# The first panel of the second output projection is accumulated inside the attention mixer's last turns, and the mixer's follow-up products come one turn later

## The chip, the cores and the metric

One of the cores of a Trainium2 chip runs the whole program. The metric is the device time of one execution in microseconds (us). TensorE (PE) does the matrix products and transposes, ScalarE (ACT), VectorE (DVE) and GpSimd (POOL) the rest, and SyncE (SP) issues most transfers. Each engine takes its instructions in the written order and waits on semaphores.

## The reference

One inference step of a decoder with two layers, for a prompt of 1024 tokens and a group of 8 sequences with 4 new tokens each (1056 tokens in all, 1024 features).

```
layer 0: h += mlstm(rmsnorm(h)) @ w_out_a        ; h += relu(rmsnorm(h) @ w_up)^2 @ w_down
k, v = rmsnorm(h) @ w_kv                         (16 heads of 64, shared)
layer 1: q = rmsnorm(h) @ w_q_b
         z = q k^T / 8 + bias, causal, strictly  (prompt: 1024 new keys;
                                                  sample: 1024 paged keys and 4 new ones)
         a[t,s] = sigmoid(z[t,s]) * prod over s<j<t of (1 - sigmoid(z[t,j]))
         y = a v ; h += y @ w_out_b              ; h += relu(rmsnorm(h) @ w_up)^2 @ w_down
y = rmsnorm(h)
```

The change touches the attention of layer 1 (the second mixer) and `y @ w_out_b`.

## The kernel before, in words

Every activation is kept with a feature to a partition, [128, 8, 1056] in float32: `m.h` is the residual, later the mixer's output y. A dense product is made from three float32r matmuls: operand and weight are each split into a high part (a cast, `w_hi`, `x_hi`) and a low part (the difference, `w_lo`, `x_lo`), and hi*hi, hi*lo and lo*hi are added up in PSUM. A weight panel has 128 output features and 1024 inputs: `load_panel` brings it into one of two buffers `w_raw`, `split_panel` (POOL, L162 and L164) splits it. A panel is worked on in three tiles of 352 tokens, each of 8 x 3 = 24 matmuls.

**`mixer_b`** (L1348) goes over 8 pairs of heads. A pair has 8 slots (`SLOTS`), one for each tile of 128 query rows, the largest first; slot number 8p+n is slot n of pair p, pairs and slots being counted from 0. In each slot PE runs `turns`: first `z(p, n, 0)` (scores of both heads, L1592 and the mask L1596), then the turns that `turns_of` lists. A turn is a set of transposes into bank 5 or 6 in alternation (`turn`), which ACT then copies out (`read_turn`); with it goes a product that uses the copy (`follow`). The kinds are "page" (cached keys, transposes L1623; after the fourth page the sample group's scores, L1673), "pack" (weights a, transposes L1642; then the product with the values, L1688), "sat" (the sample group's weights, L1649), "new", "values", "keys" and "ys" (the sample group's y, L1655). `turn` waits until the turn two before it was read. After a turn comes a part of the next pair's projections (`third`, L1576 to L1578: 6 or 9 matmuls of 352 columns), as many per slot as `THIRDS_AT` says and none in the last pair, after the second turn `z(p, n, 1)` where the tile has a second chunk, and then `follow` of the turn before. In slots 1 and 5 the product of cached values with the sample weights comes in four quarters (`values`, L1702; the last also L1707): after the turns 0, 1 and 3 and at the end of the slot. SP loads the pages into a ring of 8 buffers, in the order of their use, and each load waits until PE has used the page 8 loads ago.

ACT makes the gates of each chunk and head, two sigmoids (`gates`, L1774 and L1775), between the copies of the turns in a written order: one `gates` after each turn. It may start a slot's gates when DVE has done the last slot's. DVE (`chain_of`) does for each chunk two running products (scan, L1915) and two products of SBUF with SBUF (L1921); the sample group has its own (`chain_sample`, L1930 and L1934, in slots 3, 4, 7 and 0). PE's packs of slot n are in slot n+1 and wait for these (`a_ready`). `run_out` (L1939) copies the finished y tile from PSUM into `m.h`.

After its last slot the mixer has on SP `head_loads` (the first two panels of w_out_b) and on POOL `head_splits`.

**`out_and_mlp`** (L1978) follows behind a barrier of all engines. It splits y: for each of its 8 feature blocks k a cast on ACT (L2088) and a difference on DVE (L2142). PE waits for block k and does panel 0 (`out_matmuls`, 72 matmuls, L2032 to L2034), then the panels 1 to 7 tile by tile. ACT, after the casts, brings back the residual that had been spilled, block by block (L2092, `h_back`), and DVE adds each tile to it (L2148). Between two panels' sums DVE also adds up squares (`norm_add`) and makes the low part of the next operand (`x_low`), each after a step of ACT. A tile of panel n starts when the sum of the same tile of panel n-1 has been read (`tile_free`).

## Time and profile before

| | us |
|---|---|
| median of 3 runs | 2983.94 |
| lowest and highest | 2976.22, 2984.82 |
| the profiled execution, its own time | 2977.9 |
| its span | 2976.1 |
| PE busy | 2847.8 (96%) |
| DVE busy | 1303.7 (44%) |
| ACT busy | 819.4 (28%) |
| POOL busy | 731.6 (25%) |

All instants below are us from the start of the span of this one execution. The second mixer's pairs start at 1363.8 and the last of them at 2034.1; PE ends the mixer at 2111.1. A group of instructions is shown with its count, its busy time, the mean of one in ns, and the idle time of its engine just before it with what ended that. Matmuls overlap, so that one of 352 columns lasts some 323 ns but the next starts about 160 ns later.

### The profile page before, as it was taken

Reading aid. Unit: us, or ns where it says so; the run is one execution under the profiler, and the core shown is the slowest. Engines: PE = TensorE matmul, PEld = TensorE weight load, DVE = VectorE, ACT = ScalarE, POOL = GpSimd, SP = SyncE. Lnnn points to the kernel's source line nnn. Section 1 sums busy time; section 2 is a strip of 40 time slices with the busy share of each in tenths; the row PEclk is TensorE's granted clock in tenths of the full one; section 3 lists DMA queues with packets and bytes.
Section 4 is the critical chain, followed back from the end, with each engine's and each line's share of the span. In section 5 each row is a group of like instructions: output and inputs, shape, how many; then the busy total and the mean of one; then the engine's idle time right before and its main releaser. Section 6 shows DMA issues by size and latency. Waiting matters only on the chain. (4 is left out here: it accounts for less than half of the span.)

```text
span 2976.1 us, 49009 instructions
## 1 busy us (share of the span) xinstructions
PE 2847.8 (96%) x19713; PEld 2609.5 (88%) x19713; DVE 1303.7 (44%) x1851; ACT 819.4 (28%) x1675; POOL 731.6 (25%) x449
## 2 busy tenths in 40 slices
PE   7999998999999999999999999998899999999998
PEld 6988887999999999986777677665799999999997
DVE  6323345433333333355556655565543333333334
ACT  5221123201110011125555655556320111001112
POOL 3222102223232232322112111210222323223231
PEclk9999998999999999999999999999899999999999
DMA  5575524222323223234343443434311111111112
GB/s 164 187 148 187 100 30 102 92 86 86 98 85 99 85 89 94 86 103 120 113 121 107 115 128 108 121 101 114 123 50 43 44 49 42 49 42 47 45 43 79
DMA packets 361448, 277.23 MB, mean 93 GB/s; under 512 B 31379, under 2 KB 352915, under 8 KB 359251
## 3 DMA queue, kind: packets, MB, share of 16 engines
q1 hardware_dynamic: 340074, 261.97, 30.3%
q10 hardware_dynamic: 21224, 13.15, 2.3%
q8 instruction: 108, 1.77, 0.3%
q14 instruction: 42, 0.34, 0.0%
HBM read 251.06 MB, written 91.11 MB: 115 GB/s over the span
## 5 line engine op out<-in xcount | busy, mean ns | idle before, releaser
L162 POOL CAST w_hi<-w_raw 128x1024 fp32r<-128x1024 f32 x193 | 206.2, 1068 | 1606.8 <-PE bank L214 904.6
L212 PE MATMUL bank<-p_u_hi,w_hi 128*128 128x352 f32 x1536 | 496.6, 323 | 7.2 <-DVE p_u_lo L2166 5.8
L212 PE MATMUL bank<-x_hi,w_hi 128*128 128x352 f32 x1536 | 496.0, 323 | 1.7 <-PEq L2256 1.7
L213 PE MATMUL bank<-p_u_lo,w_hi 128*128 128x352 f32 x1536 | 495.7, 323 | 0.0
L214 PE MATMUL bank<-p_u_hi,w_lo 128*128 128x352 f32 x1536 | 495.5, 323 | 0.0
L214 PE MATMUL bank<-x_hi,w_lo 128*128 128x352 f32 x1536 | 493.8, 321 | 0.0
L213 PE MATMUL bank<-x_lo,w_hi 128*128 128x352 f32 x1536 | 493.2, 321 | 0.0
L164 POOL TENSOR_TENSOR w_lo<-w_raw,w_hi 128x1024 fp32r<-128x1024 f32 x193 | 468.2, 2426 | 15.5
L2116 ACT ACTIVATE p_u_hi<-p_relu 128x352 fp32r<-128x352 f32 x192 | 95.7, 499 | 1207.0 <-DVE p_relu L2163 1207.0
L2172 DVE TENSOR_TENSOR h<-bank,h 128x352 f32<-128x352 f32 x384 | 198.6, 522 | 467.1 <-PE bank L214 467.1
L2166 DVE TENSOR_TENSOR p_u_lo<-p_relu_sq,p_u_hi 128x352 fp32r<-128x352 f32 x192 | 229.1, 1193 | 182.7 <-ACT p_relu_sq L2117 182.7
L212 PEld LDWEIGHTS bank<-p_u_hi,w_hi 128*128 128x128 f32 x1536 | 288.4, 188 | 12.2 <-issue 10.0
L212 PEld LDWEIGHTS bank<-x_hi,w_hi 128*128 128x128 f32 x1536 | 288.5, 188 | 3.6 <-issue 3.6
L213 PEld LDWEIGHTS bank<-x_lo,w_hi 128*128 128x128 f32 x1536 | 289.3, 188 | 0.0
L214 PEld LDWEIGHTS bank<-x_hi,w_lo 128*128 128x128 f32 x1536 | 288.6, 188 | 0.0
L213 PEld LDWEIGHTS bank<-p_u_lo,w_hi 128*128 128x128 f32 x1536 | 288.5, 188 | 0.0
L214 PEld LDWEIGHTS bank<-p_u_hi,w_lo 128*128 128x128 f32 x1536 | 288.5, 188 | 0.0
L1915 DVE TENSOR_TENSOR_SCAN square<-square,zero 128x512 f32<-128x512 f32 (+5 forms) x192 | 217.9, 1149 | 150.5 <-ACT square L1775 149.1
L2163 DVE SCALAR_TENSOR_TENSOR p_relu<-bank,rms_inverse 128x352 f32<-128x352 f32 x192 | 100.0, 521 | 270.9 <-PE bank L214 263.5
L812 PE MATMUL bank<-x_hi,w_hi 128*128 128x352 f32 x576 | 200.7, 348 | 5.3 <-DVE p_v_next L1155 2.5
L814 PE MATMUL bank<-x_hi,w_lo 128*128 128x352 f32 x576 | 186.3, 323 | 0.0
L813 PE MATMUL bank<-x_lo,w_hi 128*128 128x352 f32 x576 | 186.1, 323 | 0.0
(271 smaller groups left out, 4426.6 us busy)
## 6 DMA issues: line engine op xcount, KB each, us to landing
k_pages<-in_cache_k SPq DMA_DIRECT2D x64, 512.0 KB, 5.9
w_raw<-in_w_up SPq DMA_DIRECT2D x64, 512.0 KB, 4.0
v_pages<-in_cache_v SPq DMA_DIRECT2D x64, 512.0 KB, 4.7
w_raw<-in_w_down SPq DMA_DIRECT2D x64, 512.0 KB, 3.4
p_pages<-k_pages SPq DMA_DIRECT2D x256, 128.0 KB, 2.4
p_pages<-v_pages SPq DMA_DIRECT2D x256, 128.0 KB, 2.4
w_raw<-in_w_in_a SPq DMA_DIRECT2D x25, 512.0 KB, 4.1
h_spill<-h SPq DMA_DIRECT2D x16, 528.0 KB, 5.2
```

Source lines behind the costliest of these rows:

```text
L162: pool.tensor_copy(m.whi[slot][:, :], m.wraw[slot][:, :]).then_inc(w.hi, 1)
L164: pool.tensor_tensor(m.wlo[slot][:, :], m.wraw[slot][:, :], f32(m.whi[slot][:, :]), ALU.subtract)\
L212: pe.matmul(bank[:, 0:TW], wh, xh, start=(k == 0), stop=False)
L213: pe.matmul(bank[:, 0:TW], wh, xl, start=False, stop=False)
L214: last = pe.matmul(bank[:, 0:TW], wl, xh, start=False, stop=(k == nk - 1))
L812: pe.matmul(bank[:, 0:TW], wh, xh, start=(kk == 0), stop=False)
L813: pe.matmul(bank[:, 0:TW], wh, xl, start=False, stop=False)
L814: last = pe.matmul(bank[:, 0:TW], wl, xh, start=False, stop=(kk == KT - 1))
L1915: dve.tensor_tensor_scan(stick, stick, m.zero[:, 0:1].broadcast_to([P, hi - lo]), sticks[h2][:, hi:hi + 1] if x else 1.0, ALU.mult, ALU.ad ...
L2163: dve.scalar_tensor_tensor(out=relu[t][:, :], in0=m.bank[t][:, 0:TW], scalar=0.0, in1=m.rs[:, toks], op0=ALU.max, op1=ALU.mult).then_inc(w ...
L2166: dve.tensor_tensor(ulo[:, u, toks], sqr[t][:, :], f32(uhi[:, u, toks]), ALU.subtract)\
L2172: dve.tensor_tensor(ht, m.bank[t][:, 0:TW], ht, ALU.add).then_inc(w.tile_free[t], 1)
```

## The change

In the mixer:
- `follow` of a turn comes one turn later (a list `pending`, emptied by `settle`): after the transposes of the turn two behind it. One is carried over into the next slot, behind its `z`.
- The quarters 0 and 1 of `values` both come after turn 0 of slots 1 and 5; quarter 3 goes into the next slot, after turn 1. ACT's `gates_sample` and `rows_sample` move with this.
- `head_loads` on SP moves from the end to slot 3 of the last pair (slot number 59), ahead of that slot's page loads.
- POOL, once DVE has done slot 2 of the last pair, splits w_out_b's panel 0, then the y blocks of pairs 0 to 6 (`split_y`: a cast and a difference of 128 x 1056 each, put into halves of `x_hi` and `x_lo`), then panel 1.
- PE does, for k = 0 to 6, panel 0's 9 matmuls each (`out_first`): the tiles 0 and 1 behind the last 7 turns (from turn 3 of slot 61 on), the tile 2 at the ends of the last two slots, after bank 2 is free.

In `out_and_mlp`, for the second layer alone (`begun`): PE starts with panel 1, blocks 0 to 3, in banks 3 to 5; then block 7 of panel 0; then blocks 4 to 7 of panel 1. ACT and DVE split y only for the blocks 7, 4, 5 and 6.

```
+def early_place(k):
+    return (k + KT // 2) % KT
...
-    VALUES_AFTER = {0: [0], 1: [1], 3: [2]}
+    VALUES_AFTER = {0: [0, 1], 3: [2]}
+    LAST_VALUES_AT, LAST_AFTER = {2: 0, 6: 1}, 1
...
+    OUT_FROM, OUT_K = SLOTS * (PAIRS - 1) + 5, PAIRS - 1
+    OUT_LAST_TILE = {SLOTS * PAIRS - 1: range(0, 3), SLOTS * PAIRS: range(3, OUT_K)}
...
+    OUT_SKIP = sum(len(turns_of(s)) for s in range(OUT_FROM, LAST)) - OUT_K
...
+        after = m.heads[3]
+        y_hi, y_x = own.sem("y_hi_ready"), own.sem("y_split")
...
+                if slot == OUT_FROM - 2:
+                    head_loads(eng, m, after, w, 3 * PAIRS)
                 used = len(at(KEYS_AT, slot)) * 2 * SG + len(at(VALUES_AT, slot)) * SG * QUARTERS
...
-            head_loads(eng, m, m.heads[3], w, 3 * PAIRS)
...
-            head_splits(pool, m, m.heads[3], w, (TILES * PAIRS - NT, TILES * PAIRS))
+            def split_out(slot):
+                pool.wait_ge(after.w.loaded[slot], 16)
+                split_panel(pool, m, after.w, slot, slot, None)
+            def split_y(k):
+                hi, lo = m.xhi[:, early_place(k), :], m.xlo[:, early_place(k), :]
+                pool.wait_ge(y_ok, (k + 1) * SLOTS)
+                pool.wait_ge(turn_read, TURN_NO["ys", k, 1] + 1)
+                pool.tensor_copy(hi, m.h[:, k, :]).then_inc(y_hi, 1)
+                pool.wait_ge(y_hi, k + 1)
+                pool.tensor_tensor(lo, m.h[:, k, :], f32(hi), ALU.subtract).then_inc(y_x, 1)
+            pool.wait_ge(w.tile_ready, TILES * PAIRS)
+            pool.wait_ge(a_ready, unit_no(PAIRS - 1, 3, 0, 0))
+            split_out(0)
+            for k in range(OUT_K):
+                split_y(k)
+            split_out(1)
...
+            pending = []
+            def settle(left):
+                while len(pending) > left:
+                    follow(pending.pop(0))
+            def out_first(k, tiles):
+                pe.wait_ge(y_x, k + 1)
+                if k == 0:
+                    pe.wait_ge(after.w.split, 1)
+                    pe.wait_ge(w.tile_free[0], TILES * PAIRS)
+                wh, wl = m.whi[0][:, k * P:(k + 1) * P], m.wlo[0][:, k * P:(k + 1) * P]
+                for t in tiles:
+                    bank, ts = m.bank[t][:, 0:TW], slice(t * TW, (t + 1) * TW)
+                    xh, xl = m.xhi[:, early_place(k), ts], m.xlo[:, early_place(k), ts]
+                    pe.matmul(bank, wh, xh, start=(k == 0), stop=False, skip_group_check=True)
+                    pe.matmul(bank, wh, xl, start=False, stop=False, skip_group_check=True)
+                    pe.matmul(bank, wl, xh, start=False, stop=False, skip_group_check=True)
...
-                quarters = [(q, g, x) for q, g in at(VALUES_AT, slot) for x in range(QUARTERS)]
+                outs = sum(len(turns_of(x)) for x in range(OUT_FROM, slot)) - OUT_SKIP
+                quarters = [(q, g, x) for q, g in at(VALUES_AT, slot) for x in range(QUARTERS - 1)]
                 tiles = 0 <= p < PAIRS
                 lower = tiles and len(CHUNKS[n]) > 1
                 if tiles:
                     z(p, n, 0)
-                before = None
+                settle(0)
                 for i, y in enumerate(turns_of(slot)):
                     turn(y)
+                    settle(1)
+                    pending.append(y)
                     if fill:
                         third(p, d)
                         d, fill = d + 1, fill - 1
+                    if slot >= OUT_FROM and outs + i >= 0:
+                        out_first(outs + i, (0, 1))
                     if i == 1 and lower:
                         z(p, n, 1)
-                    if before is not None:
-                        follow(before)
-                    before = y
                     for x in VALUES_AFTER.get(i, ()):
                         if x < len(quarters):
                             values(*quarters[x])
+                    if i == LAST_AFTER:
+                        for q, g in at(LAST_VALUES_AT, slot):
+                            values(q, g, QUARTERS - 1)
                 while fill:
                     third(p, d)
                     d, fill = d + 1, fill - 1
-                if before is not None:
-                    follow(before)
+                for k in OUT_LAST_TILE.get(slot, ()):
+                    if k == 0:
+                        pe.wait_ge(ys_read, PAIRS * 2)
+                    out_first(k, (2,))
+                settle(1 if 0 <= slot < SLOTS * PAIRS - 1 else 0)
                 if len(turns_of(slot)) < 2 and lower:
                     z(p, n, 1)
...
-                    if i and turns[i - 1][0] == "page" and turns[i - 1][2][2] == SG - 1:
-                        gates_sample(turns[i - 1][1], *turns[i - 1][2][:2])
+                    if i == LAST_AFTER + 1 - (turns[LAST_AFTER + 1:][:1] in [[("ys", q, g)] for q, g in at(LAST_VALUES_AT, slot)]):
+                        for q, g in at(LAST_VALUES_AT, slot):
+                            rows_sample(q, g)
+                    if i >= 2 and turns[i - 2][0] == "page" and turns[i - 2][2][2] == SG - 1:
+                        gates_sample(turns[i - 2][1], *turns[i - 2][2][:2])
                 if slot == EARLY:
...
-                if turns and turns[-1][0] == "page" and turns[-1][2][2] == SG - 1:
-                    gates_sample(turns[-1][1], *turns[-1][2][:2])
+                for y in turns[-2:]:
+                    if y[0] == "page" and y[2][2] == SG - 1:
+                        gates_sample(y[1], *y[2][:2])
                 for x, h2 in due:
                     gates(p, n, x, h2)
-                for q, g in at(VALUES_AT, slot):
-                    rows_sample(q, g)
...
-def out_and_mlp(nc, m, own, w_out, w_up, w_down, gain, gather, head, after, norm_after):
...
+        if begun:
+            yhi = [m.xhi[:, early_place(k), :] for k in range(HALF)] + [uhi[:, k - HALF, :] for k in range(HALF, KT)]
+            ylo = [m.xlo[:, early_place(k), :] for k in range(HALF)] + [ulo[:, k - HALF, :] for k in range(HALF, KT)]
+            y_order = [KT - 1] + list(range(HALF, KT - 1))
+        else:
+            yhi = [uhi[:, k, :] for k in range(HALF)] + [m.xhi[:, k, :] for k in range(HALF, KT)]
+            ylo = [ulo[:, k, :] for k in range(HALF)] + [m.xlo[:, k, :] for k in range(HALF, KT)]
+            y_order = list(range(KT))
+        def out_bank(n, t):
+            return m.bank[3 + t if begun and n == 1 else t][:, 0:TW]
...
-            pe.wait_ge(w.split, 1)
-            for k in range(KT):
-                pe.wait_ge(y_x, k + 1)
+                check = dict(skip_group_check=True) if begun and n == 0 else {}
+                pe.matmul(out_bank(n, t), wh, yhi[k][:, ts], start=(k == 0), stop=False, **check)
+                pe.matmul(out_bank(n, t), wh, ylo[k][:, ts], start=False, stop=False, **check)
+                return pe.matmul(out_bank(n, t), wl, yhi[k][:, ts], start=False, stop=(k == KT - 1), **check)
+            if begun:
+                pe.wait_ge(w.split, 2)
+                for k in range(HALF):
+                    for t in range(NT):
+                        out_matmuls(1, k, t)
+                pe.wait_ge(y_x, 1)
                 for t in range(NT):
-                    last = out_matmuls(0, k, t)
-                    if k == KT - 1:
-                        last.then_inc(w.tile_ready, 1)
-            for n in range(1, KT):
+                    out_matmuls(0, KT - 1, t).then_inc(w.tile_ready, 1)
+                pe.wait_ge(y_x, KT - HALF)
+                for t in range(NT):
+                    for k in range(HALF, KT):
+                        last = out_matmuls(1, k, t)
+                    last.then_inc(w.tile_ready, 1)
+            else:
+                pe.wait_ge(w.split, 1)
+                for k in range(KT):
+                    pe.wait_ge(y_x, k + 1)
+                    for t in range(NT):
+                        last = out_matmuls(0, k, t)
+                        if k == KT - 1:
+                            last.then_inc(w.tile_ready, 1)
+            for n in range(2 if begun else 1, KT):
                 pe.wait_ge(w.split, n + 1)
                 for t in range(NT):
...
-            for k in range(KT):
+            for k in y_order:
                 act.activation(yhi[k], m.h[:, k, :], ACT.Copy).then_inc(y_hi, 1)
             for k in range(KT):
-                act.wait_ge(y_x, k + 1)
+                if k in y_order:
+                    act.wait_ge(y_x, max(y_order.index(x) for x in y_order if x <= k) + 1 if begun else k + 1)
                 act.dma_start(m.h[:, k, :], m.spill[k]).then_inc(h_back[k], 16)
...
-            for k in range(KT):
-                dve.wait_ge(y_hi, k + 1)
+            for i, k in enumerate(y_order):
+                dve.wait_ge(y_hi, i + 1)
                 dve.tensor_tensor(ylo[k], m.h[:, k, :], f32(yhi[k]), ALU.subtract).then_inc(y_x, 1)
...
-                    dve.tensor_tensor(ht, m.bank[t][:, 0:TW], ht, ALU.add).then_inc(w.tile_free[t], 1)
+                    dve.tensor_tensor(ht, out_bank(k, t), ht, ALU.add).then_inc(w.tile_free[t], 1)
...
         phase(mixer_b)
-        phase(out_and_mlp, d["w_out_b"][0], d["w_up"][1], d["w_down"][1], m.g_mlp[1], False, m.heads[3], None, 0)
+        phase(out_and_mlp, d["w_out_b"][0], d["w_up"][1], d["w_down"][1], m.g_mlp[1], False, m.heads[3], None, 0, True)
```

## Rows read from the trace of the kernel before

**Rows 1.** The page's part 1: TensorE, its busy time, share of the span, instructions

```profile
PE 2847.8 (96%) x19713; PEld 2609.5 (88%) x19713; DVE 1303.7 (44%) x1851; ACT 819.4 (28%) x1675; POOL 731.6 (25%) x449
```

**Rows 2.** Busy time by stretch: length, then each engine's busy us (instructions); clock, DMA share, GB/s

```profile
1363.80:2034.10 670.30, 637.08 (x5542) 478.13 (x5538) 388.15 (x522) 378.86 (x797) 109.83 (x60) 1.00 0.41 117
...
2069.80:2111.20 41.40, 28.35 (x277) 17.07 (x275) 25.22 (x35) 23.15 (x54) 7.12 (x4) 0.91 0.34 95
...
2115.50:2141.20 25.70, 25.68 (x146) 25.62 (x147) 14.13 (x15) 7.56 (x8) 3.45 (x2) 0.90 0.58 210
...
2109.20:2120.40 11.20, 6.23 (x23) 5.49 (x24) 6.69 (x8) 9.05 (x10) 0.00 (x0) 0.50 0.64 202
```

**Rows 3.** TensorE's waits, pairs 0 to 6 (1363.8 to 2034.1): us, times, longest

```profile
PE bank L1688 <- ACT p_weights_t L1827: 17.6, 35, 1.0
PE bank L1702 <- DMA p_pages<-v_pages: 6.1, 7, 1.4
PE bank L1623 <- ACT p_page_keys_t L1811: 4.3, 7, 0.6
PE bank L1673 <- ACT p_page_keys_t L1811: 4.0, 7, 0.6
```

**Rows 4.** TensorE's waits in slot 2 of pair 6 (1961.7 to 1976.2)

```profile
PE bank L1688 <- ACT p_weights_t L1827: 1.1, 2, 0.8
```

**Rows 5.** ScalarE in slot 2 of pair 6, in order of time: start, duration, instruction

```profile
1968.83 0.71 ACT L1774 ACTIVATE p_weights<-bank,p_bias 128x512 f32<-128x512 f32 x1
...
1969.98 0.61 ACT L1811 COPY p_page_keys_t<-bank 128x512 f32<-128x512 f32 x1
```

**Rows 6.** GpSimd in order of time where both engines had work queued (1298 to 1305)

```profile
1298.97 1.84 POOL L162 CAST w_hi<-w_raw 128x1024 fp32r<-128x1024 f32 x1 [0.17 <-POOL w_raw L158]
1300.90 3.29 POOL L164 TENSOR_TENSOR w_lo<-w_raw,w_hi 128x1024 fp32r<-128x1024 f32 x1
```

**Rows 7.** VectorE in the same stretch

```profile
1299.84 2.08 DVE L295 TENSOR_TENSOR squares<-squares,square 128x1056 f32<-128x1056 f32 x1
```

**Rows 8.** VectorE in slot 63 (2103.3 to 2109.1), under GpSimd's two panel splits

```profile
2103.35 2.17 DVE L1915 TENSOR_TENSOR_SCAN square<-square,zero 128x127 f32<-128x127 f32 x1
...
2106.55 2.37 DVE L1921 TENSOR_TENSOR p_weights<-p_weights,square 128x127 f32<-128x127 f32 x1
```

**Rows 9.** VectorE by shape, 2066.3 to 2100.8, no GpSimd work: count, busy, mean ns

```profile
L1915 DVE TENSOR_TENSOR_SCAN square<-square,zero 128x511 f32<-128x511 f32 x4 | 4.9, 1243 | 2.0 <-ACT square L1775 2.0
L1915 DVE TENSOR_TENSOR_SCAN square<-square,zero 128x383 f32<-128x383 f32 x2 | 1.9, 956 | 2.7 <-ACT square L1775 2.7
L1930 DVE TENSOR_TENSOR_SCAN squares<-squares,zero 128x544 f32<-128x544 f32 x1 | 1.3, 1284 | 0.0
...
L1921 DVE TENSOR_TENSOR p_weights<-p_weights,square 128x511 f32<-128x511 f32 x2 | 1.3, 676 | 0.0
...
L1921 DVE TENSOR_TENSOR p_weights<-p_weights,square 128x127 f32<-128x127 f32 x2 | 0.5, 275 | 0.0
```

**Rows 10.** GpSimd's panel splits by line, 2120 to 2600

```profile
L164 POOL TENSOR_TENSOR w_lo<-w_raw,w_hi 128x1024 fp32r<-128x1024 f32 x41 | 98.6, 2404 | 3.3
L162 POOL CAST w_hi<-w_raw 128x1024 fp32r<-128x1024 f32 x41 | 42.6, 1039 | 346.0 <-PE bank L214 217.7 <-issue 83.2 <-PE bank L2034 45.1
```

**Rows 11.** SyncE's issues around slots 58 and 63, and a panel's time to landing

```profile
2068.01 0.58 SPq L1542 DMA_DIRECT2D out_v_sample<-p_v_rows  x1
...
2095.69 1.87 SPq L130 DMA_DIRECT2D w_raw<-in_w_out_b  x2
...
w_raw<-in_w_out_b SPq DMA_DIRECT2D x2, 512.0 KB, 5.8
```

**Rows 12.** The start of the output projection: PE's first matmul, panel 1's last sum, reload

```profile
2115.52 0.63 PE L2032 MATMUL bank<-p_u_hi,w_hi 128*128 128x352 f32 x1 [4.44 <-DVE p_u_lo L2142]
...
2141.19 0.52 DVE L2148 TENSOR_TENSOR h<-bank,h 128x352 f32<-128x352 f32 x1 [3.33 <-PE bank L2034]
...
h<-h_spill ACTq DMA_DIRECT2D x8, 528.0 KB, 5.5
```

9 lines of the change are left out of this document (3 added, 6 removed).

## The prediction

> **What bounds the kernel now.** I read the busy times first. TensorE is busy for 96% of the span [rows 1], so a gain must come from its idle time, from its clock, or from fewer matmuls, and none are removed here: they move. So I read by stretch [rows 2]. In the mixer's pairs 0 to 6 PE is busy 637.1 of 670.3 us: 33 us idle, nearly all of it the 32.0 us of waits listed in [rows 3], 4.6 a pair. From slot 3 of the last pair to the mixer's end it is busy only 28.4 of 41.4 us. Behind that end it stands 4.44 us until the first y block is split [rows 12], and up to 2120.4 its granted clock is 0.50, the 1.2 GHz level [rows 2]. These are the two places that the change aims at. The third view is of DVE and POOL, which make what PE would wait for next.
>
> **Part 1, the order in pairs 0 to 6.** Each group of waits asks: what is late when the waiting product is moved back?
> The DMA wait (6.1 us in 7 pairs, 0.9 each [rows 3]) is the last quarter of the cached values in slot 1. It moves behind two turns of slot 2, some 3 us later, and its pages are asked for at the same time as before or earlier. It goes: -0.9. The next key pages are released later for it, but come in 2.5 us and are due about 3 us after. I cost that at nothing; if that cover is short, up to 1 us a pair returns.
> The waits on ACT (17.6 + 4.3 + 4.0 [rows 3], 3.7 a pair) go only in part. The transposes two turns on need the same copy read as `follow` does, so the wait moves to them unless PE has more work in between or ACT is faster. In slot 2, with 1.1 us of these [rows 4] and 0.6 of L1623, ACT goes through copy, gates, copy in the written order: the gates of 1968.83 stand ahead of the copy of 1969.98 that PE waits for [rows 5]. This order stays. What PE gains is the 0.6 us of a `follow` and 1 us of the moved quarter as filling, less a `rows_sample` of 0.3 us now in ACT's queue there: I take -0.7 of 1.7. Slot 3 has most of the rest of the L1688 waits, 1.2 us, behind the same kind of gates: -0.1. In slot 6 turns with only copies on ACT lie between; its 0.8 us (0.6 of L1673, 0.2 of L1688) nearly goes: -0.7. Against it, the sample scores of pages now come after the next slot's `z`, so their gates delay the slot's own on ACT by 1 us, and `z(p, 0, 1)` waits for these: +0.3.
> Sum: -0.9 - 0.7 - 0.1 - 0.7 + 0.3 = -2.1 a pair, seven times **-15 us**. The bounds: the DMA wait alone, -6, and all waits, -32. I stay near the lower, since ACT's order decides and is not changed where most of the wait is.
>
> **Part 2, POOL's work in the last pair.** This costs more than it seems. Where DVE and POOL both have work, they take turns: POOL's cast from 1298.97 lasts 1.84 us instead of 1.04 [rows 6, 10], DVE's sum from 1299.84 lasts 2.08 and ends at 1301.92 [rows 7], 1.1 us after that cast, and POOL's difference from 1300.90 lasts 3.29 instead of 2.40: it began in earnest when DVE's sum ended. It holds for the scans too: in slot 63 a scan of 127 columns takes 2.17 us and a product 2.37 where products of this width take 0.28 [rows 8, 9], each ending as POOL's instruction ends. Copies out of PSUM aren't held.
> The Trainium skill, SBUF — State Buffer, section "Who interferes with whom", states the same as a lock held for the whole instruction, by any VectorE operation with two SBUF inputs against a GpSimd one that reads SBUF. By that rule the new work could not hide beside DVE's, only in its gaps; the rows agree.
> POOL starts when w_out_b's panel 0 has landed. SP comes to it after the store of 2068.01, so at 2068.6, and a panel takes 5.8 us [rows 11]: 2074.4. Its two issues, 1.9 us, stand ahead of slot 3's page loads, which have to wait for PE's page turns about as long anyway: nothing, or 1 us if not. From there POOL has 2 panels at 1.04 + 2.40 us and 7 y blocks, 1056 columns wide instead of 1024, at 1.07 + 2.48 [rows 10]: 6.9 + 24.9 = 31.7 us. DVE has, from the second chunk of slot 3 to the end of slot 62's chain, 10 scans and 10 products: 4 scans of 511 columns at 1.24, 2 of the sample group at 1.28, 2 of 383 at 0.96 and 2 of 255 at about 0.7, 10.8 us; the products lie between 0.68 and 0.28, some 5.9 in all [rows 9]. Of these 16.7 us neighbouring records overlap by about 0.1 each, so 14.7 us of holding. Both in turn: 2074.4 + 31.7 + 14.7 = 2120.8. Slot 62's chain ended just before 2103.35 [rows 8]: 17 us later. DVE's gaps don't save this: POOL always has the next instruction ready, and 31.7 + 14.7 us exceed the 29 us there were.
> What follows on the end of that chain: before 7.8 us (2103.3 to 2111.1), of which POOL's panels cost 4 [rows 8] that is now gone. New on this path are matmuls. Of the 63 moved, at 0.16 us, 10.1 us in all, most stand where PE waits anyway; but the 6 and 12 of slot 64 (2.9 us) and a few in slot 62, with the moved quarter and the copy that the "ys" turn then waits for, come after the last chains: +4.5. PE's new waits on y blocks (`y_x`) cost nothing, since POOL is through with a block before DVE has the chain that the same turn needs. The two pieces cancel nearly; the earlier slots of the pair gain 0.8 by part 1's order. Last pair: **+17 us**, with bounds of +3 (all of POOL's work in gaps: only the tail's matmuls) and +22 (every POOL instruction on the path).
> The clock: it fell to 0.50 around waits of 3.4 and 4.4 us at the end [rows 2, 12]. Now PE waits about 4 us twice in slots 60 to 62, and works 20 us in between; I take 5 to 6 us of that work at the half clock with half of it on the path: **+3** (0 to +10).
>
> **Part 3, the projection's start.** Before: from PE's last mixer matmul at 2111.1 (2115.52 less 4.44) to the end of panel 1 at 2141.1 [rows 12] 30.0 us: the wait, 144 matmuls at 0.16, and 2.4 for the slow clock. After: the barrier, 0.6, then 36 + 9 + 36 = 81 matmuls, 13.0: the needed y block 7 is split after 3 us, beside these. The four casts and four differences of y that ACT and DVE no longer make lay beside PE's work: nothing. That alone gives 13.6. But next is late the residual. Its reload is issued only behind four casts, about 5.9 us after the mixer, and takes 5.5 [rows 12]: 11.4. Then DVE has 3 sums of 0.52, ACT a square, DVE an addition and a low part, some 5 us, before panel 1's first sum frees the tile that panel 2 waits for: 17.1. Part 3: 17.1 - 30.0 = **-13 us**; bounds -16.4 (nothing late) and -11.
>
> **Sum.** -15 + 17 + 3 - 13 = -8 us. Against the profiled execution, 2977.9 us, that is 2970; against the median of the runs, 6 us higher, 2976.
>
> **The rivals.**
> A, POOL's work hides. If DVE regains its delays in the 16 us for which it is idle in the last 41 [rows 2], the pair grows by some 5 instead of 20: -15 + 5 - 13 = -23, 2961. For it: DVE does wait for ACT and PE there. Against it: the sum above leaves no gap unused. 0.18.
> B, the order pays more. If two further copies' waits go in slots 2 and 3, part 1 is -25: 2966. For it: PE gets one more turn's work before each wait. Against it: ACT's gates stand between. 0.12.
> C, slower. The last pair starves PE so long that its clock stays at the half level from slot 60 into the projection. Then the 25 us of PE work there take up to twice as long and cover DVE no more: +10 on top of +3, and if the order gives just the DMA waits, -6: -6 + 17 + 13 - 13 = +11, 2995. It decides from about 10 us of half clock on the path. For it: the clock fell after waits of this size. 0.15.
> D, part 1 does not do what it says: the waits move to the transposes entire, and the key pages' wait replaces the values'. Then 0 + 17 + 3 - 13 = +7, 2991. 0.10.
> The forecast has 0.45, over some 2969 to 2984.
>
> **How the numbers follow.** A measurement of this kernel tells 0.3%, 9 us, from no change: faster is below 2975, slower above 2993. Of the forecast's 0.45 I count 0.15 as faster and 0.30 as same; A and B are faster (0.30); C is slower (0.15); D lies by the edge, 0.07 same and 0.03 slower. Faster 0.45, same 0.37, slower 0.18. The range, 2957 to 2996, takes in A, B, D and most of C.
>
> **What would show it.** Right: PE's waits in pairs 0 to 6 near 17 us, no L1702 wait on DMA, L1642 or L1623 in its place; POOL busy without a break from about 2060 on for 45 us; scans and products of slots 59 to 62 at 2 to 3 us; the last pair 90 us and more long; panel 2 of the projection waiting for `tile_free`. Wrong: the last pair under 82 us, or scans that keep their 1.2 us beside POOL; waits of pairs 0 to 6 below 8 us or above 26.

## The result and the profile after

| | before | after |
|---|---|---|
| median of 4 runs, us | 2981.93 | 2949.96 |
| lowest and highest, us | 2976.22, 2984.82 | 2949.24, 2953.85 |
| the profiled execution, its own time, us | 2977.9 | 2949.79 |
| its span, us | 2976.1 | 2948.0 |

The ratio is 0.9898, with a 95% interval of 0.988 to 0.9916. The kernel is faster by 1%, some 30 us. The prediction gave "faster" a chance of 0.45; its 2976 us and its range from 2957 us on both miss: every term of the sum came out lower, none above what was forecast.

In the stretches of the prediction, each cut at the same instruction in both traces (the first `z` of pair 0, that of pair 7, PE's last product of the mixer, the first matmul of the projection's panel 2), in us:

| stretch | before | after | difference | predicted |
|---|---|---|---|---|
| ahead of the second mixer's pairs | 1363.8 | 1361.6 | -2.2 | 0 |
| pairs 0 to 6 | 670.3 | 647.3 | -23.0 | -15 |
| last pair | 77.0 | 89.6 | +12.6 | +17 and +3 |
| mixer's end to panel 2 | 29.9 | 14.1 | -15.8 | -13 |
| the rest | 827.0 | 827.3 | +0.3 | 0 |

The stretches sum to the difference of the spans, 28.1 us. The first one is no effect: over the traces of all kernels of this case it lies between 1361.0 and 1366.2 with nothing in it changed.

One of these boundaries does not part the same work in both kernels. The `follow` that is now carried over a slot's end takes 8 matmuls (sample scores, 1.0 us) from pair 6 into pair 7. Before, they start ahead of the boundary (2034.1), and after, behind it (2008.9):

```profile
2033.12 1.06 PE L1673 MATMUL bank<-p_page_keys_t,p_q_sample 128*32 128x512 f32 x8
```

```profile
2010.16 1.07 PE L1704 MATMUL bank<-p_page_keys_t,p_q_sample 128*32 128x512 f32 x8
```

So 1.0 us of the -23.0 is not saved but stands in the last pair, and the same work changed by -22.0 and +11.6.

Part 1 of the page of after:

```profile
PE 2839.9 (96%) x19713; PEld 2610.2 (89%) x19713; DVE 1343.1 (46%) x1847; ACT 815.7 (28%) x1671; POOL 766.3 (26%) x463
```

Its busy time by stretch, with the columns of [rows 2]:

```profile
1361.60:2008.90 647.30, 631.38 (x5536) 480.76 (x5532) 411.09 (x520) 378.50 (x797) 110.11 (x60) 1.00 0.42 120
2008.90:2098.50 89.60, 68.58 (x597) 43.77 (x596) 69.47 (x66) 48.04 (x103) 40.62 (x18) 0.90 0.31 86
2098.50:2112.60 14.10, 13.24 (x82) 12.92 (x82) 10.16 (x12) 7.45 (x7) 3.45 (x2) 1.00 0.85 306
```

The matmuls are the same 19713 as in [rows 1]. PE's idle time of pairs 0 to 6 halved, from 33.2 us [rows 2] to 15.9. In the last pair POOL is busy for 40.6 us, and VectorE's busy time is 69.5 us. The same 66 instructions take 48.9 us in a kernel without the y splits on POOL (order alone, below). The projection's start has hardly any idle time left and the full clock, where [rows 2] had 0.50.

PE's waits in pairs 0 to 6 after, with the columns of [rows 3]:

```profile
PE bank L1654 <- ACT p_page_keys_t L1872: 7.1, 14, 0.8
PE bank L1673 <- ACT p_weights_t L1888: 6.9, 7, 1.0
PE bank L1623 <- ACT square L1836: 1.6, 6, 0.3
PE bank L1733 <- DMA p_pages<-v_pages: 0.2, 1, 0.2
```

L1654 are the transposes of pages (L1623 before), L1673 those of the weights (L1642 before), L1623 the scores (L1592 before), L1733 the cached values (L1702 before). The 17.6 us of `follow` (L1688 [rows 3]) and the DMA wait are gone; what remains stands on transposes and scores. It is 15.8 us in all.

### The profile page after: what moved, and what is told of

It reads as the page before. It is cut to its first block and busy times, and to the rows that moved or that the text cites. A ratio compares the mean times of both kernels' runs of the same rounds, so it can differ in the third digit from the quotient of the medians.

```text
span 2948.0 us, 49024 instructions
## 1 busy us (share of the span) xinstructions
PE 2839.9 (96%) x19713; PEld 2610.2 (89%) x19713; DVE 1343.1 (46%) x1847; ACT 815.7 (28%) x1671; POOL 766.3 (26%) x463
## 5 line engine op out<-in xcount | busy, mean ns | idle before, releaser
L212 PEld LDWEIGHTS bank<-p_u_hi,w_hi 128*128 128x128 f32 x1536 | 288.7, 188 | 12.2 <-issue 10.0
L1978 DVE TENSOR_TENSOR_SCAN square<-square,zero 128x512 f32<-128x512 f32 (+5 forms) x192 | 240.9, 1277 | 92.3 <-ACT square L1836 92.0
```

The source lines that it names most:

```text
L212: pe.matmul(bank[:, 0:TW], wh, xh, start=(k == 0), stop=False)
L1978: dve.tensor_tensor_scan(stick, stick, m.zero[:, 0:1].broadcast_to([P, hi - lo]), sticks[h2][:, hi:hi + 1] if x else 1.0, ALU.mult, ALU.ad ...
```

## The experiments

The edits are against the changed kernel, but for loads early, which is against the kernel before. A comparison with the kernel before is with runs on the same chip. The stretches were cut as above, in one trace for each kernel. "Lower clock" is the time in the last pair for which PE was granted the lower level (1.2 GHz, 0.50 in the rows); what PE does in it would take half as long at the full one, so that a difference in this column is a rival for a part of a difference in the column before it.

| kernel | median | ratio to before, 95% | pairs 0 to 6 | last pair | lower clock | to panel 2 |
|---|---|---|---|---|---|---|
| before | 2981.9 to 2983.9 | | 670.3 | 77.0 | 17.9 | 29.9 |
| after | 2949.96 | 0.988 to 0.9916 | 647.3 | 89.6 | 17.1 | 14.1 |
| order alone | 2955.73 | 0.9892 to 0.9925 | 647.8 | 78.0 | 15.6 | 29.4 |
| panel alone | 2979.76 | 0.9981 to 1.0 | 673.7 | 90.9 | 23.9 | 14.1 |
| part ahead of `follow` | 2951.01 | 0.9877 to 0.991 | 646.1 | 89.5 | 17.1 | 14.2 |
| quarters back | 2969.21 | 0.9938 to 0.9973 | 661.8 | 92.1 | 23.9 | 14.1 |
| last quarter back | 2961.82 | 0.9896 to 0.9939 | 655.0 | 92.6 | 23.9 | 14.2 |
| y splits of 8 columns | 2942.56 | 0.9847 to 0.9887 | 647.3 | 78.5 | 6.8 | 14.1 |
| loads early | 2981.22 | 0.9981 to 1.0 | 671.3 | 75.6 | 17.1 | 29.2 |
| y splits sooner | 2962.86 | 0.991 to 0.9946 | 647.3 | 101.9 | 37.5 | 14.1 |
| y splits in halves | 2948.94 | 0.9867 to 0.9904 | 647.3 | 85.6 | 17.1 | 14.2 |
| cast by ACT | 2951.53 | 0.9863 to 0.9914 | 647.3 | 91.6 | 23.9 | 14.2 |
| y splits by ACT and DVE | 2948.16 | 0.9847 to 0.9892 | 647.4 | 85.6 | 17.1 | 14.2 |
| and panels later | 2946.47 | 0.9863 to 0.9896 | 647.7 | 83.3 | 17.1 | 14.2 |
| and one y moved | 2946.64 | 0.9862 to 0.9895 | 647.3 | 82.2 | 13.7 | 14.1 |

**One part each.** The order alone leaves out the panel's part:

```
-                if slot == OUT_FROM - 2:
-                    head_loads(eng, m, after, w, 3 * PAIRS)
...
+            head_loads(eng, m, m.heads[3], w, 3 * PAIRS)
...
-            split_out(0)
-            for k in range(OUT_K):
-                split_y(k)
-            split_out(1)
+            head_splits(pool, m, m.heads[3], w, (TILES * PAIRS - NT, TILES * PAIRS))
...
-                    if slot >= OUT_FROM and outs + i >= 0:
-                        out_first(outs + i, (0, 1))
...
-        phase(out_and_mlp, d["w_out_b"][0], d["w_up"][1], d["w_down"][1], m.g_mlp[1], False, m.heads[3], None, 0, True)
+        phase(out_and_mlp, d["w_out_b"][0], d["w_up"][1], d["w_down"][1], m.g_mlp[1], False, m.heads[3], None, 0, False)
```

> Part 1 alone: the turn order, the quarters and ScalarE's order as in the changed kernel; w_out_b's first panels, the y splits and panel 0 as in the kernel before. Theory 1 (the gain is the order's; the early panel gives back in the last pair what it takes from the projection): 25 to 30 us below the kernel before, so about 2953, pairs 0 to 6 in 647 us as in the changed kernel, the last pair 72 to 75. Theory 2 (each part pays about half, as the change is laid out): 12 to 18 us below, about 2966, since without the early panel the gain of 16 us at the projection's start is missing.

Measured: 2955.73 us, and 647.8 us for pairs 0 to 6. The order gives all of that stretch's gain, as the first theory has it. The last pair is 1.0 us longer, neither 72 to 75 us nor 0.8 shorter as forecast; the 8 matmuls that now lie behind the boundary are that 1.0 us.

The panel alone has the old order of `follow`, `values` and the gates:

```
-    VALUES_AFTER = {0: [0, 1], 3: [2]}
+    VALUES_AFTER = {0: [0], 1: [1], 3: [2]}
...
-                    settle(1)
-                    pending.append(y)
                     if fill:
                         third(p, d)
...
                     if i == 1 and lower:
                         z(p, n, 1)
+                    settle(0)
+                    pending.append(y)
...
-                settle(1 if 0 <= slot < SLOTS * PAIRS - 1 else 0)
+                settle(0)
```

> Part 2 alone: the order of turns, follow-ups and quarters as in the kernel before; the head loads in slot 59, the y splits on GpSimd, panel 0 in the last turns and the new start of the projection as in the changed kernel. Theory 1: within 5 us of the kernel before: pairs 0 to 6 at 670 us, the last pair 13 to 17 us longer (90 to 94), the projection's start 16 shorter. Theory 2: 10 to 16 us below it.

Measured: 2979.76 us, within 5 us of the kernel before, as in the first theory. The projection's start pays 15.8 us, the last pair takes 13.9 of it back, and what is left is not told from nothing (0.9981 to 1.0). Pairs 0 to 6 are 3.4 us longer here. PE was at the lower level for 10.2 us of them, where before was for 3.4, which makes 3.4 us if PE was busy throughout, as it was:

```profile
1363.10:2036.90 673.80, 640.19 (x5544) 480.95 (x5540) 387.69 (x522) 379.51 (x797) 109.79 (x60) 0.99 0.41 116
```

**What in the order pays.** Three edits. First, the `third` ahead of the `follow` again, everything else as in after:

```
-                    settle(1)
-                    pending.append(y)
                     if fill:
                         third(p, d)
...
                     if slot >= OUT_FROM and outs + i >= 0:
                         out_first(outs + i, (0, 1))
+                    settle(1)
+                    pending.append(y)
```

> The changed kernel, but the follow-up product (still two turns late) stands behind the part of the projections instead of ahead of it. In pairs 0 to 6 TensorE's waits fell by 16 us and the time by 23. Theory 1 (the other 7 us are the order of matmul shapes: a follow-up behind a part starts 0.25 us after its predecessor, one behind a transpose 0.20, and a part behind a transpose has a slow second matmul): pairs 0 to 6 take 5 to 7 us more, 652 to 654, with waits unchanged near 16 us. Theory 2 (the 7 us are waits that the profile doesn't list): no change, 645 to 649.

Measured: 646.1 us against 647.3, with the waits on ACT the same to a tenth. Which of the two comes first is not the reason.

Second, all quarters of `values` and the copy of the sampled rows go back to their old places:

```
-    VALUES_AFTER = {0: [0, 1], 3: [2]}
+    VALUES_AFTER = {0: [0], 1: [1], 3: [2]}
...
-                quarters = [(q, g, x) for q, g in at(VALUES_AT, slot) for x in range(QUARTERS - 1)]
+                quarters = [(q, g, x) for q, g in at(VALUES_AT, slot) for x in range(QUARTERS)]
...
-                    if i == LAST_AFTER:
-                        for q, g in at(LAST_VALUES_AT, slot):
-                            values(q, g, QUARTERS - 1)
...
+                for q, g in at(VALUES_AT, slot):
+                    rows_sample(q, g)
```

> The changed kernel with the four quarters of the cached values where they were (turns 0, 1, 3 and the slot's end). Theory 1 (the quarters' move takes away the DMA wait of 0.9 us a pair and fills ScalarE's wait in slot 2): 8 to 12 us slower than the changed kernel, with 6 us or more of waits on value pages. Theory 2 (the later follow-ups alone did it, since they leave the pages more time): 0 to 3 us slower.

Measured: 661.8 us, so that the quarters' move is 14.5 of the 23.0 us and the later `follow` the other 8.5, of which 1.0 is the work that now lies behind the boundary and 1.7 the clock (next section). PE's waits there, with the columns of [rows 3]:

```profile
PE bank L1673 <- ACT p_weights_t L1884: 12.6, 14, 1.0
PE bank L1733 <- DMA p_pages<-v_pages: 7.7, 9, 1.7
PE bank L1654 <- ACT p_page_keys_t L1868: 5.9, 14, 0.6
PE bank L1623 <- ACT square L1832: 1.6, 6, 0.3
```

The later `follow` took the waits on ACT from 25.9 us [rows 3] to 20.1; the DMA wait stood. The quarters then take 7.5 from the DMA wait and 4.5 from those on ACT. The forecast had the DMA wait, and of the filling only a part.

Third, only the last quarter goes back, the others stay moved:

```
-                quarters = [(q, g, x) for q, g in at(VALUES_AT, slot) for x in range(QUARTERS - 1)]
+                quarters = [(q, g, x) for q, g in at(VALUES_AT, slot) for x in range(QUARTERS)]
...
-                    if i == LAST_AFTER:
-                        for q, g in at(LAST_VALUES_AT, slot):
-                            values(q, g, QUARTERS - 1)
...
+                for q, g in at(VALUES_AT, slot):
+                    rows_sample(q, g)
```

> The changed kernel, but the fourth quarter of the values' page goes back to the end of its own slot, with the copy that reads the sampled rows; quarters 0 and 1 stay behind the first turn and quarter 2 behind the fourth. Putting the whole page back cost 14.5 us of the pairs 0 to 6. Theory 1 (the quarter is needed as filling behind the next slot's first turns): the wait on the value tile's transfer stays gone, but that slot's turns wait as before, so pairs 0 to 6 take about 655 us, with 8 us of the 14.5 lost. Theory 2 (only the quarter's distance from its transfer matters, and quarters 0 and 1 behind the first turn bring it): 647 to 650 us and a kernel within 3 us of the changed one. Theory 3 (the last quarter carries it all, the wait on the transfer too): about 661 us, and some 14 us slower than the changed kernel.

Measured: 655.0 us, the time of the first theory, but not with its waits:

```profile
PE bank L1673 <- ACT p_weights_t L1884: 12.6, 14, 1.0
PE bank L1654 <- ACT p_page_keys_t L1868: 5.9, 14, 0.6
PE bank L1733 <- DMA p_pages<-v_pages: 3.9, 5, 1.2
PE bank L1623 <- ACT square L1832: 1.6, 6, 0.3
```

The DMA wait is halved and not gone, and the waits on ACT are those of the kernel with all quarters back. So the quarters 0 and 1 together behind turn 0 are worth 6.8 us, with 3.8 of it in the DMA wait. The last quarter is worth 7.7: it takes away the other 3.7 of that wait, and 4.5 of ACT's by its work in the next slot.

Most of the 3.0 us that the quarters 0 and 1 give beyond the wait is PE's own time. Two quarters next to each other take less than two apart. The first two rows are of before, the third of after (slot 1 of pair 6):

```profile
1952.13 0.65 PE L1702 MATMUL bank<-p_pages,p_weights_sample_t 128*32 128x128 f32 x16
1955.92 0.64 PE L1702 MATMUL bank<-p_pages,p_weights_sample_t 128*32 128x128 f32 x16
```

```profile
1930.97 1.08 PE L1733 MATMUL bank<-p_pages,p_weights_sample_t 128*32 128x128 f32 x32
```

A quarter alone holds the next instruction's start for 0.58 us (to 1952.71 and 1956.49), and the two together for 1.01 (to 1931.98): 0.15 less, and this 14 times in the 7 pairs, 2.0 us. By the records the 896 matmuls of pairs 0 to 6 are busy for 36.07 us before, 36.08 with all quarters back, and 33.17 with the last quarter back and in after.

**What the last pair costs.** The y splits with 8 columns keep each of POOL's 18 instructions and each semaphore, but leave 14 of them next to no work (the other columns of the split y are left out):

```
-                pool.tensor_copy(hi, m.h[:, k, :]).then_inc(y_hi, 1)
+                pool.tensor_copy(hi[:, 0:8], m.h[:, k, 0:8]).then_inc(y_hi, 1)
-                pool.tensor_tensor(lo, m.h[:, k, :], f32(hi), ALU.subtract).then_inc(y_x, 1)
+                pool.tensor_tensor(lo[:, 0:8], m.h[:, k, 0:8], f32(hi)[:, 0:8], ALU.subtract).then_inc(y_x, 1)
```

> The changed kernel, but GpSimd splits only the first 8 of the 1056 columns of each y block, so that panel 0 is accumulated from y parts that are mostly left out; the 63 matmuls stay. Order alone has a last pair of 78.0 us, with the early panel it has 89.6. Theory 1 (GpSimd's 14 instructions block VectorE's chain, the matmuls lie in waits): the last pair falls to 77 to 81 us, the scans of slots 60 to 62 take 1.3 us or less, total near 2939. Theory 2 (the 10.1 us of moved matmuls lengthen TensorE's own way): it stays at 86 to 89.

Measured: 2942.56 us and a last pair of 78.5, 11.1 less than after. What the last pair pays is the length of POOL's y splits. A part of it goes by the clock: after was at the lower level for 10.3 us more, and PE busy for 6.3 of them, so that this is 3.1 us at most. The order alone has 78.0, so the 63 matmuls moved in cost 0.5 us net of two changes that help this kernel: the panels' splits are no longer at the pair's end (loads early, below, is 1.4 us shorter than before), and PE was at the lower level for 8.8 us less. The matmuls by themselves were not measured. VectorE by shape and then POOL by shape in the changed kernel, 2048.4 to 2090.6 (count, busy, mean ns, idle before):

```profile
L1978 DVE TENSOR_TENSOR_SCAN square<-square,zero 128x511 f32<-128x511 f32 x4 | 8.2, 2067 | 2.0 <-ACT square L1836 2.0
L1978 DVE TENSOR_TENSOR_SCAN square<-square,zero 128x383 f32<-128x383 f32 x2 | 4.6, 2354 | 0.0
L1984 DVE TENSOR_TENSOR p_weights<-p_weights,square 128x511 f32<-128x511 f32 x2 | 4.3, 2191 | 0.0
...
L1993 DVE TENSOR_TENSOR_SCAN squares<-squares,zero 128x544 f32<-128x544 f32 x1 | 3.5, 3499 | 0.0
```

```profile
L1582 POOL TENSOR_TENSOR x_lo<-h,x_hi 128x1056 fp32r<-128x1056 f32 x7 | 19.8, 2828 | 0.6
L1580 POOL CAST x_hi<-h 128x1056 fp32r<-128x1056 f32 x7 | 12.2, 1743 | 0.0
L164 POOL TENSOR_TENSOR w_lo<-w_raw,w_hi 128x1024 fp32r<-128x1024 f32 x2 | 5.8, 2887 | 0.2
L162 POOL CAST w_hi<-w_raw 128x1024 fp32r<-128x1024 f32 x2 | 3.3, 1651 | 88.0 <-DMA w_raw<-in_w_out_b 88.0
```

Scans of 1243 and 956 ns [rows 9] became 2067 and 2354, a product of 676 became 2191, and POOL's casts of 1039 [rows 10] 1743. The sampled group's scan went from 1284 to 3499. POOL has 0.8 us of idle time in these 42 us and VectorE 2.0, and both are slowed.

The loads early, in the kernel before: `head_loads` at slot 59 in place of the end, nothing else. POOL's two panel splits come earlier with it.

> The kernel before with one edit: the loads of w_out_b's two first panels go to slot 59, so that their splits run there instead of in slots 62 and 63. Theory 1 (two panel splits block VectorE for some 4 us at the tail where nothing hides it, while in slot 59 TensorE has other work for part of it): the last pair 2 to 5 us shorter than 77.0. Theory 2 (the blocking only moves): within 1.5 us.

Measured: 2981.22 us, which is not told from before (0.9981 to 1.0), and in the trace a last pair of 75.6 in place of 77.0. Loads and splits together cost nothing there; what each does was not parted.

The y splits sooner: POOL makes six y blocks from slot 56 on, ahead of panel 0.

```
-            pool.wait_ge(a_ready, unit_no(PAIRS - 1, 3, 0, 0))
+            for k in range(OUT_K - 1):
+                split_y(k)
             split_out(0)
-            for k in range(OUT_K):
-                split_y(k)
+            split_y(OUT_K - 1)
             split_out(1)
```

> The changed kernel with GpSimd's y splits of pairs 0 to 5 as soon as x_hi is free, at the last pair's first slot instead of behind slot 58's chain; then panel 0, block 6, panel 1. The same instructions, started 39 us earlier. Theory 1 (what counts is that 31 us of GpSimd and VectorE's chain don't fit into the 42 us from slot 59 on): the last pair 4 to 8 us shorter, 82 to 86, since slots 56 to 58 have gaps to take some of it. Theory 2 (every blocked scan delays the chain wherever it stands): 88 to 91.

Measured: 2962.86 us, the last pair 101.9 us, 12.3 more than after; neither theory has that. There the scans of 512 columns went in pairs of 5.38 us, and slot 57 took 24.3 us in place of 9.1. So the work is not hidden further ahead either: in the changed kernel's largest slots VectorE has the least idle time (with the y splits of 8 columns it was busy 11.4 of slot 56's 12.5 us). Two things add to it. PE was at the lower level for 27.3 us from 2018.1 on and busy for 14.2 of them, up to 7.1 us. And slot 60 was hardly relieved: the six POOL instructions that were left (2064.3 to 2078.1) stood over VectorE's chain there, and it took 16.1 us in place of 17.1.

The y splits in halves: each of the 14 in two instructions of 528 columns.

```
-                pool.tensor_copy(hi, m.h[:, k, :]).then_inc(y_hi, 1)
-                pool.wait_ge(y_hi, k + 1)
-                pool.tensor_tensor(lo, m.h[:, k, :], f32(hi), ALU.subtract).then_inc(y_x, 1)
+                for i in range(2):
+                    cs = slice(i * T // 2, (i + 1) * T // 2)
+                    pool.tensor_copy(hi[:, cs], m.h[:, k, cs]).then_inc(y_hi, 1)
+                    pool.wait_ge(y_hi, 2 * k + i + 1)
+                    pool.tensor_tensor(lo[:, cs], m.h[:, k, cs], f32(hi)[:, cs], ALU.subtract).then_inc(y_x, 1)
...
-                pe.wait_ge(y_x, k + 1)
+                pe.wait_ge(y_x, 2 * (k + 1))
```

> The changed kernel with each y block split in two halves of 528 columns, so twice as many GpSimd instructions of half the length. Theory 1 (each VectorE operation waits for one GpSimd instruction, whichever runs, so the delay goes by the length of an instruction): scans of slots 60 to 62 take about 2 us instead of 3, the chain is through earlier, the last pair 3 to 8 us shorter, 82 to 87. Theory 2 (only the sum of both engines' holding counts, as in the prediction's sum): no shorter, 89 to 91, with 14 more starts.

Measured: the last pair 85.6 us, 4.0 less, with as much time at the lower clock, as the first theory has it: a VectorE instruction waits for one of POOL's at a time, so that shorter ones hold it less. The kernel's 2948.94 us is not told from 2949.96. This is a row of that kernel (2048 to 2090), where after had 2191 ns:

```profile
L1986 DVE TENSOR_TENSOR p_weights<-p_weights,square 128x511 f32<-128x511 f32 x2 | 2.7, 1414 | 0.0
```

**Off POOL.** ScalarE makes the seven casts, at the end of the slots that `SPLITS_AT` names, and POOL the differences:

```
+    SPLITS_AT = {57: [0], 58: [1], 59: [2], 60: [3], 61: [4, 5], 62: [6]}
-                pool.tensor_copy(hi, m.h[:, k, :]).then_inc(y_hi, 1)
...
+                for kb in SPLITS_AT.get(slot, ()):
+                    act.wait_ge(w.tile_ready, TILES * PAIRS)
+                    act.wait_ge(y_ok, (kb + 1) * SLOTS)
+                    act.activation(m.xhi[:, early_place(kb), :], m.h[:, kb, :], ACT.Copy).then_inc(y_hi, 1)
```

> The changed kernel, with the casts of the seven y panels on ScalarE at the end of slots 57 to 62, and their differences still on GpSimd. GpSimd's instructions in the alternation fall from 18 to 11. Theory 1 (the loss goes with the number and length of GpSimd's instructions that stand against VectorE's): the 12.1 us of GpSimd's casts no longer stop anything, so the last pair takes 84 to 86 us in place of 89.6, and the kernel about 2945 us. Theory 2 (VectorE is slowed as long as GpSimd is busy with anything, and it is the panels' own sequence that ends late): the differences wait for their y panel in each slot and reach into more scans, 87 to 92 us, and the kernel 2948 to 2953 us.

Measured: 91.6 us, 2 more than after, so the first theory falls: fewer instructions on POOL do not make the pair shorter by themselves. VectorE's busy time did fall, from 69.5 to 59.8 us. But the seventh cast comes at the end of slot 62, and POOL's last split now stands over the last chain. First POOL, then VectorE:

```profile
2089.31 2.43 POOL L1582 TENSOR_TENSOR x_lo<-h,x_hi 128x1056 fp32r<-128x1056 f32 x1 [2.07 <-ACT x_hi L1942]
2091.69 1.17 POOL L162 CAST w_hi<-w_raw 128x1024 fp32r<-128x1024 f32 x1
2092.93 2.34 POOL L164 TENSOR_TENSOR w_lo<-w_raw,w_hi 128x1024 fp32r<-128x1024 f32 x1
```

```profile
2091.10 2.03 DVE L1982 TENSOR_TENSOR_SCAN square<-square,zero 128x127 f32<-128x127 f32 x2 [1.00 <-ACT square L1836]
2093.05 2.58 DVE L1988 TENSOR_TENSOR p_weights<-p_weights,square 128x127 f32<-128x127 f32 x2
```

From the `z` of slot 63 to the mixer's end it takes 11.3 us, where after takes 7.8. PE waits 1.93 us there for the last of these products, and is at the lower level for 3.4 us behind it; in after it has neither. So it matters which of VectorE's instructions are stopped, and not only how many. The pair had 6.8 us more at the lower level than after's in all, and PE was busy in it for 6.9 us more, up to 3.4 us of time; how the 2 us part between that and the blocking is not shown.

With the differences on VectorE too, at the end of the same slots, POOL has only the two panels:

```
+                for kb in SPLITS_AT.get(slot, ()):
+                    dve.wait_ge(y_hi, kb + 1)
+                    dve.wait_ge(turn_read, TURN_NO["ys", kb, 1] + 1)
+                    dve.tensor_tensor(m.xlo[:, early_place(kb), :], m.h[:, kb, :], f32(m.xhi[:, early_place(kb), :]),
+                                      ALU.subtract).then_inc(y_x, 1)
```

> The changed kernel, with the seven y panels of the last pair split by ScalarE (the cast, at the end of slots 57 to 62) and VectorE (the difference behind it), in place of GpSimd, whose splits stopped VectorE's scans and products. GpSimd then splits only the two panels of the weights. Theory 1 (what costs is the blocking between GpSimd and VectorE, as the run with y parts of eight columns bore out with a last pair of 78.5 us): seven casts of about 1.0 us and seven differences of about 1.25 us have room in the engines' idle time, the last pair takes 79 to 82 us in place of 89.6, and the kernel 2940 to 2943 us, below both. Theory 2 (VectorE has no room at the end of these slots, and what it takes lies on the path): the 8.8 us more of VectorE come back in full, 87 to 90 us for the last pair, and 2947 to 2951 us.

Measured: 85.6 us for the last pair, between the two theories. The trace shows one reason. Without the y blocks the panels' splits stand over slot 59's chain. POOL, then VectorE:

```profile
2053.74 1.04 POOL L162 CAST w_hi<-w_raw 128x1024 fp32r<-128x1024 f32 x1 [88.80 <-DMA w_raw<-in_w_out_b]
2054.86 3.19 POOL L164 TENSOR_TENSOR w_lo<-w_raw,w_hi 128x1024 fp32r<-128x1024 f32 x1
2057.99 1.96 POOL L162 CAST w_hi<-w_raw 128x1024 fp32r<-128x1024 f32 x1
2060.04 2.68 POOL L164 TENSOR_TENSOR w_lo<-w_raw,w_hi 128x1024 fp32r<-128x1024 f32 x1
```

```profile
2056.26 2.86 DVE L1973 TENSOR_TENSOR_SCAN square<-square,zero 128x511 f32<-128x511 f32 x1 [0.36 <-ACT square L1827]
2059.05 4.22 DVE L1979 TENSOR_TENSOR p_weights<-p_weights,square 128x512 f32<-128x512 f32 x2
```

So each panel's split got a later wait, behind slot 60's and slot 61's products:

```
-            pool.wait_ge(a_ready, unit_no(PAIRS - 1, 3, 0, 0))
+            pool.wait_ge(a_ready, unit_no(PAIRS - 1, 5, 0, 0))
             split_out(0)
+            pool.wait_ge(a_ready, unit_no(PAIRS - 1, 6, 0, 0))
             split_out(1)
```

> The kernel with the y splits on ScalarE and VectorE (last pair 85.6 us), and GpSimd's splits of the two weight panels each a wait later: the first behind slot 60's products, the second behind slot 61's. In the run before they took GpSimd from 2053.7 to 2062.7 us, over slot 59's scans and products, which took 2.86 and 4.22 us for one and two instructions in place of 1.28 and 1.26 to 2.3. Theory 1 (the panels' splits are what is left of the cost): slots 59 and 60 fall from 10.3 and 14.1 us to 9.4 and 10 to 11, the last pair to 80 to 82 us, and the kernel to 2943 us or less. Theory 2 (the added casts and differences themselves lie on the path): the last pair stays at 84 to 86 us, or rises as the first matmuls of the second output projection wait for the panel, and the kernel stays at 2948 us.

Measured: 83.3 us, and 2946.47. The same instructions of VectorE there:

```profile
2056.54 1.28 DVE L1974 TENSOR_TENSOR_SCAN square<-square,zero 128x511 f32<-128x511 f32 x1 [0.36 <-ACT square L1828]
2057.74 1.27 DVE L1980 TENSOR_TENSOR p_weights<-p_weights,square 128x512 f32<-128x512 f32 x2
```

These rows are 4.5 us shorter (7.08 less 2.55), and the pair is 2.3 us shorter, with as much time at the lower clock, so that it lies between the theories. Slot 59 kept its length (10.4 us against 10.3); slot 60 went from 14.1 to 12.2, and slot 61 from 9.4 to 8.9. The third y block moved from slot 59 to 58 (`58: [1, 2]`):

> As the run with the panels' splits later, and the third y panel's cast and difference at the end of slot 58, where VectorE had 5.1 us of idle time, in place of slot 59, where the difference of 1.25 us stood between two sampled scans. Theory 1 (VectorE's 1.25 us there lie on the path of slot 60): the last pair 1 to 1.5 us shorter than in the run before. Theory 2 (they do not; ScalarE's second cast at the end of slot 58 holds up slot 59's gates by as much): no change, or 0.5 to 1 us longer.

Measured: 82.2 us, 1.1 less. That is the first theory's number, but this trace also had 3.4 us less at the lower level, with PE busy for 3.8 us less in it, which can be all of it; and the medians, 2946.64 and 2946.47, do not tell the two kernels apart. The move is not shown to pay. Of the 3.7 us left to the 78.5 of the y splits of 8 columns, up to 3.2 may be the clock. These are both last pairs, the latter's first:

```profile
2008.90:2087.40 78.50, 65.56 (x597) 42.38 (x596) 48.04 (x66) 47.81 (x103) 16.81 (x18) 0.96 0.34 98
```

```profile
2013.50:2095.70 82.20, 68.41 (x597) 43.84 (x596) 53.82 (x73) 54.65 (x110) 6.82 (x4) 0.92 0.33 94
```

They were at the lower level (1.2 GHz) for 6.8 and 13.7 us, and PE was busy in it for 5.7 and 12.1: 6.4 us more, at half the speed. How much of these lies on the path was not tried. Nor is 78.5 us a floor: that kernel still has a panel's split over slot 59's scans.

These last two kernels compute the whole and stand 3.4 us below the changed one by their medians (2946.5 and 2946.6 against 2949.96). Their last pairs are 6.3 and 7.4 us shorter, and their stretches ahead of the mixer, 1365.2 and 1366.2 us, were 4 us longer in the traces. The intervals of the ratios (0.9863 to 0.9896 and 0.988 to 0.9916) overlap, so that this is likely, not shown.

## Why the prediction missed

**What bounds the kernel: right.** Nearly the whole gain is idle time and clock in the two places named, and the matmuls are as many.

**Part 1, -15, measured -23.0.** The waits were sized rightly: 32.0 less 15 is 17, and 15.8 were left. They went where the text said: 0.2 us of wait on the DMA, and L1642 and L1623 (now L1673 and L1654) in its place. The step that failed is an unwritten one, that a stretch changes only by its listed waits. PE's busy time in it fell too, from 637.1 us [rows 2] to 631.4. The sum of both is -21.9, and 1.1 more is idle time that no wait lists (33.2 less 32.0 before, 0.1 after). The 5.7 us of busy time are these:
- 1.7 us are the clock. Before, 3.4 us from 1482.2 on were at the lower level, and after has none in these pairs. All three traces with the old order have such stretches in pairs 0 to 6 (3.4, 3.4 and 10.2 us), and none of the twelve with the `follow` later.
- 1.0 us is the 8 matmuls that lie behind the boundary, and no gain.
- 2.0 us are the quarters 0 and 1 next to each other.
- For the other 1.0 us no view names a cause.

Without the clock's part, half of the time at the lower level, the three kernels of the old order have 635.1 to 635.5 us, and the nine of the changed one 631.2 to 631.5, so the fall is the order's and not the execution's.

By its parts: the DMA wait, -0.9 a pair, was right, and went for two reasons, half by each pair of moved quarters. The move of the quarters in all measured 2.1 us a pair, where the DMA wait and what of the 0.7 in slot 2 was put to filling make 1.6 at most. What is left of the forecast for the later `follow` is 0.5 a pair, 3.8 us in all, and that measured 8.5. This is the term that was further off: 5.8 us of waits on ACT went by it (25.9 to 20.1), and the DMA wait grew by 1.6. Rival B has nearly the number, 25 for 23.0, but by copies' waits that did not go: what is left of the waits is what was forecast. D falls.

**Part 2, +17 and +3, measured +12.6.** The mechanism was right, by the run with y splits of 8 columns: 11.1 us by POOL's y splits against VectorE, with what they do to the clock, 0.5 by the moved matmuls, panels and clock together, and 1.0 by the 8 matmuls from pair 6. POOL's start was too: 40.3 us after the pair's start in the forecast (2074.4 less 2034.1), 40.2 measured (2049.1 less 2008.9). Three sizes were off.
- The alternation was to take 31.7 + 14.7 = 46.4 us and took 41.9, from POOL's start to VectorE's last product of slot 62 at 2091.0. POOL's alone is 31.7, so VectorE's 20 instructions held it for 10.2 us, 0.5 each where 0.74 were taken. The term that failed is the holding of one instruction: it is less than its length (16.7 us for 20, 0.84 each), by some 0.2 us more than the 0.1 allowed for. What VectorE does in those 0.3 us was not tried.
- The tail after that chain was to grow from 7.8 to 8.3 us and took 7.5. The 4.5 us for matmuls behind it were 0.8 too much. Against that, the 0.8 us that the earlier slots were to gain did not come.
- The clock's +3 did not come: the last pair had 17.9 us at the lower level before and 17.1 after, and the projection 9.4 and none.

The low stretches, with the columns of [rows 2], the two of before first:

```profile
2038.60:2048.80 10.20, 9.18 (x46) 4.53 (x46) 7.05 (x10) 5.83 (x14) 0.00 (x0) 0.50 0.01 2
2103.40:2120.50 17.10, 8.11 (x35) 6.57 (x34) 12.59 (x12) 10.26 (x13) 5.29 (x3) 0.50 0.43 135
```

```profile
2017.30:2024.10 6.80, 5.78 (x23) 3.18 (x23) 4.53 (x7) 4.05 (x10) 0.00 (x0) 0.50 0.01 2
2061.70:2071.90 10.20, 6.11 (x32) 3.48 (x29) 10.17 (x5) 2.01 (x4) 10.04 (x5) 0.50 0.00 0
```

A new stretch of 10.2 us came in slot 60, as forecast; PE was busy for 6.1 of it, so it cost 3.1 us at most. But the 17.1 us of before, 7.7 of them at the pair's end and 9.4 in the projection's start, kept the full clock. All twelve kernels with the moved panel have none of the lower level in the projection's start, and the three without it (before, order alone, loads early) have 6.8 to 9.4 us. Whether it is the moved matmuls or the shorter wait behind the mixer that keeps it was not parted. The forecast counted what the clock would take in slots 60 to 62 and not what it would give back. C falls with it: it came to no lower clock in the projection.

A falls as well: POOL's work hides only in part, 25 us more of it cost 11.1, where A has 5 for the pair. What would show the forecast wrong, a pair under 82 us or scans of 1.2, did not come; the pair's 90 us (89.6) and the scans and products of 2 to 3 us did. POOL was busy without a break for 41.3 us, in place of 45.

The Trainium skill, SBUF — State Buffer, section "Who interferes with whom", says of the ports that the two engines share: "Issue order, not op shape, decides who blocks." The trace agrees in that both engines were slowed (676 to 2191 ns and 1039 to 1743), and the halves bear out that a block ends with the instruction. The prediction took the lock to last for the whole instruction. That section of the Trainium skill writes this of VectorE's two-port modes, and of two SBUF inputs that they contend; here some 0.3 us of each such instruction did not block.

**Part 3, -13, measured -15.8.** Before was right with 30.0 for 29.9. After has 14.1 where 17.1 were forecast. The failed step is "issued only behind four casts, about 5.9 us after the mixer": it was issued 1.9 us after it. ScalarE's own work and its DMA issues, and then VectorE:

```profile
2100.38 1.09 ACT L2177 ACTIVATE p_u_hi<-h 128x1056 fp32r<-128x1056 f32 x1
2100.39 1.00 ACTq L2182 DMA_DIRECT2D h<-h_spill  x2
2101.37 1.07 ACT L2177 ACTIVATE p_u_hi<-h 128x1056 fp32r<-128x1056 f32 x1
```

```profile
2106.18 1.38 DVE L2238 TENSOR_TENSOR h<-bank,h 128x352 f32<-128x352 f32 x3
```

The issue stands behind the casts in the code, yet it went out with the first of them. The first sums start 7.7 us after the mixer's end, where 11.4 was taken. Then the reload is no later than VectorE itself: the quickest of the eight transfers took 5.7 us, which from 2100.39 is 2106.1, and VectorE's own four differences ended at 2106.27. From the first sums to the end it took 6.4 us where 5.7 were taken (of which the written terms, 5 and one sum of 0.52, give 5.5). So PE waits for `tile_free` only this long; the sign that the text named, a wait there, came with next to nothing:

```profile
2112.59 0.40 PE L2107 MATMUL bank<-x_hi,w_hi 128*128 128x352 f32 x1 [0.24 <-DVE h L2238]
```

**The sum.** 8.0 us were missed in part 1, 7.4 in part 2 with the clock, 2.8 in part 3 and 2.2 ahead of the mixer, 20.4 of the 20.1 between -8 and -28.1 (the rest's +0.3). The median was also 6 us above the profiled execution before and not after (2949.96 against 2949.79). All erred to one side. The 2.2 us ahead of the mixer are chance. The range's low end came from rivals taken one at a time, 2961 and 2966, and three terms off by 3 to 8 us in the same direction lie below it.

## What to carry to other kernels

Size the gain of an edit by the stretch's length between two instructions, not by its listed waits alone: here 16 us of waits came with 7 more that no list had. Then count each kind of instruction on both sides of the boundary, since 1 us of these 7 had only moved behind it. Work given to GpSimd beside VectorE's chains of two-operand instructions costs, and what it costs goes by which of VectorE's instructions it meets; so place it behind a chain, in short pieces, or give it to other engines where they have room. An edit that fills PE's idle time just ahead of a dense stretch can give the clock of that stretch back as well, and this belongs in the sum. And look at the time at the lower clock before a difference of a few us between two traces is given to an edit.

## What was not expected of the hardware

- A transfer that ScalarE issues behind four casts in the code was issued 0.01 us after the first of them began (2100.39, 2100.38), as it waited for none of them. Issue and activation of this engine do not queue for each other here.
- VectorE and GpSimd took turns through 38 instructions and 42 us. Each of VectorE's held GpSimd for some 0.5 us of its mean 0.84, and cutting GpSimd's instructions in halves gave 4.0 of 11.1 us back.
- Two quarters of 16 matmuls of 128 columns took 1.08 us next to each other and 0.65 us each apart: 0.15 us less for the two, by the start of the next instruction (1.01 in place of 2 x 0.58). In pairs 0 to 6 this is 2.0 us that no wait shows.
